# Two matmul orders changed: interleaved first tiles in the MLP's down stages, and the output stage's first row sums and projections placed behind the attention

## The chip, the cores and the metric

The kernel runs on one core of a Trainium2 chip. The metric is the device time of one execution in microseconds, the median over runs. Engines: TensorE (PE in the profile, its weight loads PEld), VectorE (DVE), ScalarE (ACT), GpSimd (POOL) and SyncE (SP), which issues the DMAs. They work in parallel, each through its own list in order, and wait for each other by semaphores.

## What is computed

One transformer block over 1024 tokens of width 1024 (float32), with 256 context tokens for keys and values only:

```python
sh1, sc1, g1, sh2, sc2, g2 = modulation(c, w_mod, b_mod)
mix_lat = concatenate([mla_latent(...), swa_latent(...)])   # 8 full heads, 8 windowed heads
x = x + g1 * (mix_lat @ w_out)
x = x + g2 * squared_relu_mlp(modulate(x, g_mlp, sh2, sc2), w_mlp1, w_mlp2)

def squared_relu_mlp(h, w1, w2):
    a = jax.nn.relu(h @ w1)
    return (a * a) @ w2
```

`modulate` is an RMS norm with a gain, times (1 + scale), plus shift. The softmax of the attention is divided by its row sum; the kernel does this late, on the mixed output.

## The kernel before, in words

Each float32 operand of the large products is split into a high and a low half (fp32r): high by ScalarE (a copy), low by VectorE (value minus high). A product takes three matmuls: high x high, high x low, low x high. PSUM has eight banks of 128 x 512.

**Attention** (`attention_phase`). Steps s = 0 to S - 1 (S = 96), the last 64 for the full heads: one head and one tile of 128 queries. In a step TensorE makes the scores (L1347), VectorE their negated maximum (L1542), ScalarE the exponentials (L1467), TensorE turns them (L1363, three fills of 4, 4 and 2 tiles, through the two banks TB = 0, 1), ScalarE and VectorE split each fill (L1453, L1548), and TensorE multiplies with the values (L1391, bank 7), once for two steps. The fills pass a ring of two banks: fill n waits for `emptied` n - 1. TensorE's list for step s: scores of s with the third fill of s - 2 between them, fills 0 and 1 of s - 1, half of the values of unit (s - 3) // 2.

**Row sums.** `rs` holds the reciprocal row sums of a token tile. GpSimd widens a tile's (`widen`, L1677), TensorE turns them (L1685, two banks of four transposes), VectorE multiplies the mixed output with them (`scale_mix`, L1690), ScalarE and VectorE split the product (`high_mix` L1695, `low_mix` L1700) and TensorE projects it (`project`, L1715, 2 halves of 24 matmuls). In the kernel before, tiles 0 and 1 are turned inside the attention's ring at steps S - 3 and S - 2 (`TURN`), which gives the ring four more slots; the first half of tile 0's projection stands in TensorE's list ahead of the last step's fills and the second half behind them. The reciprocals are ready in two groups (`full_sums`): tiles 0 and 1 at step S - 4, tiles 2 to 7 behind the last attention output.

**Output stage** (`out_phase`). For tile t TensorE's list is: turn the row sums of t + 2, project t + 1, turn the normed tile t (L1820). VectorE's list is: gate and residual of t (L1773, L1777), the norm, `scale_mix` and `low_mix` of t + 2, then gain, shift and low half of the normed tile (L1792 to L1798).

**MLP** (`mlp_phase`). FF = 4096 in 32 blocks of 128; 8 stages of FC = 4 blocks. A stage has four up products (L2045, 48 matmuls each over all 1024 tokens), and eight down products, one for each token tile t (`down`, L2059, 4 blocks x 3 x 2 halves = 24 matmuls). Between them ScalarE rectifies and squares (L1985, L1987), VectorE squares and takes the low half (L2009, L2012). Tile t of the down stage uses the bank pair DB[t % 2] and waits until VectorE has added tile t - 2's pair to the accumulator (`added`, L2028; `finished`, L2026, in the last stage). Tile 0 waits ahead of each block f for `a_ready` and `w2_ready` of that block. The middle six stages are a loop. GpSimd multiplies the second weights with the gate (L1955).

Of the kernel before, what the change touches and what calls it, by code (L numbers as in the profile page):

```python
# [1029 lines left out]
def attention_phase(nc, A, scr, Z, tok, prep, me):  # L1030
# [138 lines left out]
    def hi_count(s, k):  # L1169

        return fill0[s] + k + 1

    def turn_slot(s, f):

        return slot(s - 1, 1) + 1 + f
# [116 lines left out]
    def tensor():  # L1292
# [112 lines left out]
        def turn_sums(s, t):  # L1405

            for f in range(2):
                n = turn_slot(s, f)
                pe.wait_ge(emptied, n - 1)
                prep.turn_sums(ps[:, TB + n % 2, :], t, f).then_inc(filled, 1)  # L1410
# [39 lines left out]
    def scalar():  # L1450
# [36 lines left out]
        for s in range(S + 1):  # L1487
# [15 lines left out]
            else:  # L1503
# [24 lines left out]
    def vector():  # L1528
# [16 lines left out]
        def lo_fill(s, k):  # L1545
            dve.wait_ge(hi_ready, hi_count(s, k))
            hi, lo = hi_lo(s, k)
            V.tensor_tensor(lo, turned(s, k), hi.bitcast(F32), ALU.subtract).then_inc(emptied, 1)  # L1548
# [28 lines left out]
        def scale_mix(s, t):  # L1577

            for f in range(2):
                n = turn_slot(s, f)  # L1580
                dve.wait_ge(filled, n + 1)
                prep.scale_mix(ps[:, TB + n % 2, :], t, f).then_inc(emptied, 1)

        for s in range(S + 1):
# [28 lines left out]
            if s - 1 in TURN:  # L1613
                prep.low_mix(TURN[s - 1])
# [4 lines left out]
    me.turn_done, me.sums_done, me.out_done, me.units = (filled, turn_slot(S - 2, 1) + 1), (rs_ready, 2), out_done, U  # L1619
# [6 lines left out]
def out_phase(nc, A, scr, Z, att, mlp, me):  # L1626
# [19 lines left out]
    TB, BB = 0, (4, 7)  # L1646
    YB = (2, 5)
# [31 lines left out]
    def turn_sums(to, t, f):  # L1679

        if f == 0:
            pe.wait_ge(widened, t + 1)
        for c in range(4):
            k = 4 * f + c
            last = nc.tensor.transpose(to[:, c * P:(c + 1) * P], flat(rb[:, 2 * k:2 * k + 2, :]), ident[:, :])  # L1685
        return last

    def scale_mix(src, t, f):

        return V.tensor_tensor(mn[:, t % 2, 1, 4 * f:4 * f + 4, :], src.rearrange("p (k c) -> p k c", k=4),  # L1690
                               mix[:, 4 * f:4 * f + 4, tile(t)], ALU.mult)

    def high_mix(t):

        nc.scalar.activation(mT[:, t % 2, 0, :, :], mn[:, t % 2, 1, :, :], ACT.Copy).then_inc(m_hi, 1)  # L1695
# [7 lines left out]
    def project(t, half):  # L1703

        if half == 0:
# [3 lines left out]
            if t == 1:  # L1709
                pe.wait_ge(att.exped, att.steps)  # L1710
# [17 lines left out]
    def sync():  # L1728
        sp.wait_ge(att.out_done, att.units)
        sp.dma_start(g1[:, :, :], scr["mod"][0:1, 2 * D:3 * D].partition_broadcast(P).rearrange("p a (k c) -> p (a k) c", c=P)).then_inc(g1_loaded, 16)  # L1730
        for t in range(NB):
            if t == NB - 1:
                sp.wait_ge(spread, 2 * (NB - 2))
                mlp.sync_first()
# [4 lines left out]
    def gpsimd():  # L1739
        for t in range(2, NB):  # L1740
            if t == 2:
                pool.wait_ge(*att.turn_done)
                pool.wait_ge(*att.sums_done)
            else:
                pool.wait_ge(spread, 2 * (t - 2))
            widen(t)

    def scalar():
        for t in range(NB):
# [6 lines left out]
            if t + 2 < NB:  # L1756
                act.wait_ge(scaled, 2 * t + 2)
# [6 lines left out]
    def vector():  # L1764
        dve.wait_ge(columns, 48)
        link(V.tensor_scalar_add(mcol[:, 1, :], mcol[:, 1, :], 1.0))
        link(V.tensor_tensor(mcol[:, 1, :], mcol[:, 1, :], gcol[:, :], ALU.mult))
        dve.wait_ge(g1_loaded, 16)
        for t in range(NB):
# [13 lines left out]
            if t + 2 < NB:  # L1783
                for f in range(2):
                    dve.wait_ge(spread, 2 * t + f + 1)
                    scale_mix(ps[:, BB[f], :], t + 2, f).then_inc(scaled, 1)
# [14 lines left out]
    def tensor():  # L1801
        def spread_sums(t):

            for f in range(2):
                if t == 2 and f == 1:
                    pe.wait_ge(att.out_done, att.units)
                if t > 2:
                    pe.wait_ge(scaled, 2 * (t - 3) + f + 1)
                turn_sums(ps[:, BB[f], :], t, f).then_inc(spread, 1)

# [12 lines left out]
        pe.wait_ge(att.exped, att.steps)  # L1823
        for t in range(NB):
# [5 lines left out]
            else:  # L1830
                pe.wait_ge(gated, NB - 1)
# [3 lines left out]
        pe.wait_ge(scaled, 2 * (NB - 2))  # L1835
        mlp.up_half(1, 0)
        pe.wait_ge(gated, NB)
# [4 lines left out]
    me.widen, me.turn_sums, me.scale_mix, me.high_mix, me.low_mix, me.project = widen, turn_sums, scale_mix, high_mix, low_mix, project  # L1842
# [4 lines left out]
def mlp_phase(nc, A, scr, Z, o, out, me):  # L1847
# [189 lines left out]
    def tensor():  # L2037
# [11 lines left out]
        def down(n, t, g0, free):  # L2049
            b = DB[t % 2]  # L2050
            if free is not None:
                pe.wait_ge(*free)
            for f in range(FC):
                if t == 0:
                    pe.wait_ge(a_ready, g0 + f + 1)
                    pe.wait_ge(w2_ready, g0 + f + 1)
                for i, (x, w) in enumerate(((0, 0), (0, 1), (1, 0))):
                    for half in range(2):
                        last = nc.tensor.matmul(ps[:, b + half, :], aT[x][:, f, t * P:(t + 1) * P],  # L2059
                                                w2[w][:, f, half * BANK:(half + 1) * BANK],  # L2060
                                                start=(f == 0 and i == 0), stop=(f == FC - 1 and i == 2))
            last.then_inc(down_ready, 1)
# [3 lines left out]
        for t in range(NB):  # L2066
            down(t, t, 0, (o.scaled_h, 2 * NB) if t < 2 else (added, t - 1))
        with pe.Fori(1, NCH - 1) as ch:
            for f in range(FC):
                up(ch * FC + f, f)  # L2070
            for t in range(NB):
                down(ch * NB + t, t, ch * FC, (added, ch * NB + t - 1))
# [3 lines left out]
        for t in range(NB):  # L2076
            down(n0 + t, t, NF - FC, (added, n0 + t - 1) if t < 2 else (finished, 2 * t - 2))
# [138 lines left out]
```

## Time and profile before

| | us |
|---|---|
| median of 3 runs | 1503.82 (1502.24 to 1505.94) |
| the profiled execution | 1506.07 |
| its span, first to last instruction | 1504.2 |
| TensorE busy | 1409.5 (94%) |
| VectorE busy | 834.0 (55%) |
| ScalarE busy | 611.9 (41%) |
| GpSimd busy | 390.4 (26%) |
| down products, 1536 matmuls (L2059) | 351.6 |
| up products in the loop and tail, 1440 matmuls (L2045) | 327.8 |
| projections, 384 matmuls (L1715) | 91.9 |

The attention ends near 688 us of the span, the output stage near 800, and the MLP takes the rest. Busy time says how long an engine has work in it; what ends a wait is in the chain of waits and the timeline. TensorE's matmul durations overlap, so for it the distance between starts counts, and the granted clock (1.0 is 2.4 GHz, 0.5 is 1.2 GHz).

### The profile page before, as it was taken

What the parts mean: (1) busy time and instruction counts of PE and PEld (TensorE: products, weight loads), DVE (VectorE), ACT (ScalarE), POOL (GpSimd) and SP (SyncE); (2) the same over time, 40 slices, a digit from 0 to 9 for tenths busy, and PEclk for the clock granted to TensorE, in tenths of its full rate; (3) what the DMA queues carried; (4) which work ended last, traced back from release to release, by engine and by line L of the source; (5) the groups of instructions that cost most, each with busy time, mean ns of one, the idle gap of its engine ahead of it and who ended that gap; (6) DMA issues with size and microseconds to landing.
All of it is one profiled execution on the core that took longest, in us unless ns stands there. A gap on an engine that the chain in (4) does not pass through costs nothing.

```text
span 1504.2 us, 19176 instructions
## 1 busy us (share of the span) xinstructions
PE 1409.5 (94%) x7467; PEld 1186.4 (79%) x7467; DVE 834.0 (55%) x1143; ACT 611.9 (41%) x1194; POOL 390.4 (26%) x270
## 2 busy tenths in 40 slices
PE   3699997999999999988998999999999999999998
PEld 0488886888899998977877887887878788787887
DVE  1667786788788877864775325242343424344332
ACT  2455655777777787952223112030211203021120
POOL 4345653000099991301002111020110201011010
PEclk9999998999999999999999999999999999999999
DMA  9456657900156536201023111020201102011012
GB/s 332 136 146 175 177 149 242 276 12 1 66 165 204 161 115 178 66 1 55 30 70 98 42 56 57 28 84 0 84 28 47 65 13 91 8 58 53 28 56 98
DMA packets 123347, 141.03 MB, mean 94 GB/s; under 512 B 10224, under 2 KB 105216, under 8 KB 120464
## 3 DMA queue, kind: packets, MB, share of 16 engines
q1 hardware_dynamic: 122768, 140.08, 30.2%
q8 instruction: 44, 0.72, 0.2%
q14 instruction: 23, 0.19, 0.0%
q0 software_dynamic: 512, 0.04, 0.0%
HBM read 108.37 MB, written 31.74 MB: 93 GB/s over the span
## 4 chain that ended last, share of the span: by engine, by line
PE 71%; DVE 14%; ACT 9%; DMA 3%; issue 2%; SPq 1%; POOL 0%; DVEq 0%; ACTq 0%; POOLq 0%
PE f_ps L2045 22%; PE f_ps L2059 21%; PE a_ps L1347 7%; PE a_ps L1363 5%; PE a_ps L1391 5%; ACT s_pr L1459 2%; PE t_ps L923 2%; PE o_ps L1715 2%; DMA t_wm<-in_w_mod 2%; ACT s_pT L1453 2%; PE t_ps L912 2%; DVE f_aT L2012 1%; DVE s_nmx L1537 1%; PE t_ps L935 1%; DMA scratch_sv<-t_vs 1%
## 5 line engine op out<-in xcount | busy, mean ns | idle before, releaser
L2059 PE MATMUL f_ps<-f_w,f_aT 128*128 128x512 f32 x1536 | 351.6, 390 | 10.6 <-DVE f_aT L2012 9.8
L2059 PEld LDWEIGHTS f_ps<-f_w,f_aT 128*128 128x128 f32 x1536 | 287.8, 188 | 73.1 <-DVE f_aT L2012 12.3
L2045 PE MATMUL f_ps<-h,f_w 128*128 128x512 f32 x1440 | 327.8, 389 | 0.5 <-DVE f_w L1903 0.5
L2045 PEld LDWEIGHTS f_ps<-h,f_w 128*128 128x128 f32 x1440 | 270.2, 188 | 56.9 <-DVE f_w L1903 0.9
L1955 POOL TENSOR_TENSOR f_w2r<-f_w2r,f_g 128x1024 f32<-128x1024 f32 x32 | 81.6, 2550 | 620.2 <-DMA f_w2r<-in_w_mlp 620.2
L2028 DVE TENSOR_TENSOR mix<-mix,f_ps 128x512 f32<-128x512 f32 x112 | 71.9, 684 | 216.0 <-PE f_ps L2059 216.0
L2009 DVE TENSOR_TENSOR f_a<-f_r 128x1024 f32<-128x1024 f32 x32 | 55.5, 1735 | 187.2 <-ACT f_r L1985 187.2
L1972 ACT ACTIVATE f_w<-f_w2r 128x1024 fp32r<-128x1024 f32 x32 | 33.7, 1052 | 300.8 <-PE f_ps L2059 295.0
L1548 DVE TENSOR_TENSOR l_pT<-a_ps,l_pT 128x512 fp32r<-128x512 f32 (+1 forms) x192 | 108.9, 594 | 65.0 <-ACT l_pT L1453 65.0
L1347 PE MATMUL a_ps<-l_k,l_q 96*128 96x512 f32 (+1 forms) x576 | 136.4, 366 | 0.5 <-DVE l_mo L1569 0.5
L923 PE MATMUL t_ps<-w_in,t_h 128*128 128x416 f32 (+2 forms) x624 | 127.4, 350 | 1.5 <-DVE t_h L711 1.5
L1985 ACT ACTIVATE f_r<-f_ps 128x1024 f32<-128x1024 f32 x32 | 32.9, 1029 | 230.2 <-PE f_ps L2045 221.7
L1453 ACT ACTIVATE l_pT<-a_ps 128x512 fp32r<-128x512 f32 (+1 forms) x192 | 95.0, 525 | 54.1 <-PE a_ps L1363 53.9
L923 PEld LDWEIGHTS t_ps<-w_in,t_h 128*128 128x128 f32 x624 | 101.9, 189 | 7.8 <-issue 1.7
L1467 ACT ACTIVATE l_pr<-a_ps,l_nb 128x256 f32<-128x256 f32 (+1 forms) x128 | 100.6, 791 | 15.1 <-DVE l_nb L1542 12.7
L1347 PEld LDWEIGHTS a_ps<-l_k,l_q 96*128 96x128 f32 x576 | 95.3, 189 | 12.4 <-DVE l_mo L1569 0.7
L1542 DVE TENSOR_REDUCE l_nb<-a_ps 128x1 f32<-128x1280 f32 x64 | 94.9, 1482 | 4.0 <-PE a_ps L1347 3.6
L1363 PE MATMUL a_ps<-ident,l_pr 128*128 128x128 f32 x640 | 93.9, 275 | 3.0 <-DVE l_pT L1548 2.9
L1715 PE MATMUL o_ps<-o_w,o_mT 128*128 128x512 f32 x384 | 91.9, 399 | 2.6 <-DVE o_mT L1700 2.6
L1391 PE MATMUL a_ps<-l_pT,l_v 128*128 128x256 f32 x640 | 91.4, 290 | 2.0 <-DVE mix L1562 1.5
L1363 PEld LDWEIGHTS a_ps<-ident,l_pr 128*128 128x128 f32 x640 | 73.7, 140 | 18.3 <-DVE l_pT L1548 9.2
L1715 PEld LDWEIGHTS o_ps<-o_w,o_mT 128*128 128x128 f32 x384 | 73.1, 192 | 18.7 <-DVE o_mT L1700 3.5
(205 smaller groups left out, 1889.9 us busy)
## 6 DMA issues: line engine op xcount, KB each, us to landing
l_wg<-in_w_mod SPq DMA_DIRECT2D x8, 2048.0 KB, 8.5
f_w1r<-in_w_mlp SPq DMA_DIRECT2D x32, 512.0 KB, 4.0
f_w2r<-in_w_mlp SPq DMA_DIRECT2D x32, 512.0 KB, 4.5
t_wm<-in_w_mod SPq DMA_DIRECT2D x8, 1024.0 KB, 8.6
scratch_k<-t_kT SPq DMA_DIRECT2D x20, 384.0 KB, 4.4
l_k<-scratch_k SPq DMA_DIRECT2D x8, 960.0 KB, 10.6
scratch_q<-t_qT SPq DMA_DIRECT2D x16, 384.0 KB, 4.8
l_q<-scratch_q SPq DMA_DIRECT2D x8, 768.0 KB, 7.3
```

The lines of the kernel that those rows point to most:

```text
L923: ins = MM(ps[:, ZB + n % 2, 0:w], hT[a][:, k, :], w_in[x][:, k, ZC[c]], start=(k == 0 and i == 0), stop=(k == KC - 1 and i == 2))
L1347: last = MM(fps[:, a0:a0 + hi - lo], qT[b][:, a, qt * P:(qt + 1) * P], kT[b][:, w, lo:hi], start=(i == 0), stop=(i == 2))
L1363: last = nc.tensor.transpose(ps[:, TB + n % 2, c * P:(c + 1) * P], x, ident[:, :])
L1391: last = MM(ps[:, OB, 0:2 * P], vm[h % 2][:, t, :], flat(l_pT[half][:, u % 2, t, :, :]), start=(half == 0 and t == 0), stop=(half == 1 and ...
L1453: nc.scalar.activation(hi_lo(s, k)[0], turned(s, k), ACT.Copy).then_inc(hi_ready, 1)
L1467: nc.scalar.activation(l_pr[:, odd, lo:hi], fps[:, a0 + lo:a0 + hi], ACT.Exp, bias=nb[:, odd:odd + 1], accum_out=l_sums[:, i, m % NB, m // ...
L1542: V.tensor_reduce(nb[:, s % 2:s % 2 + 1], fps[:, (s % 2) * KALL:(s % 2 + 1) * KALL], AX.X, ALU.max, negate=True).then_inc(shift_ready, 1)
L1548: V.tensor_tensor(lo, turned(s, k), hi.bitcast(F32), ALU.subtract).then_inc(emptied, 1)
L1715: last = nc.tensor.matmul(ps[:, YB[t % 2] + half, :], mT[:, t % 2, a, k, :], w_out[w][:, k, half * BANK:(half + 1) * BANK], start=(k == 0 ...
L1955: nc.gpsimd.tensor_tensor(w2r[:, :], w2r[:, :], g2[:, :], ALU.mult).then_inc(w2_gated, 1)
L2045: last = nc.tensor.matmul(ps[:, b + half, :], w1[:, slot, w, k, :], h2[x][:, k, half * BANK:(half + 1) * BANK], start=(k == 0 and i == 0), ...
L2059: last = nc.tensor.matmul(ps[:, b + half, :], aT[x][:, f, t * P:(t + 1) * P], w2[w][:, f, half * BANK:(half + 1) * BANK], start=(f == 0 an ...
```

## The change

In the down stages (`down_first`) TensorE makes blocks 0 to 2 of tile 0, blocks 0 to 2 of tile 1, then block 3 of tile 0 and block 3 of tile 1. Tiles 2 to 7 are as before. Before block 3 it waits for the block's `a_ready` and `w2_ready` as before.

In the attention the two `TURN` insertions go, and with them the ring's four extra slots and tile 0's projection halves at the last step. Tile 0's row sums are turned behind the last third fill, ahead of the last values, into the output stage's own pair of banks 2 and 3 (`spread_sums(0)`). Tile 1's are turned behind the last values, and then tile 0 is projected in one piece, ahead of the output stage's loop. VectorE's and ScalarE's shares of tile 0 stand ahead of the last attention output, those of tile 1 behind the last reciprocals. Projections use the pairs 4, 5 and 6, 7 in place of 2, 3 and 5, 6. The numbers of some waits follow.

The core of the diff:

```diff
@@ attention_phase @@
-    TURN = {S - 3: 0, S - 2: 1}
     def slot(s, k):
-        return fill0[s] + k + sum(2 for x in TURN if x <= s or (x == s + 1 and k == 2))
+        return fill0[s] + k
@@ attention_phase, gpsimd @@
-        for t in range(2):
-            if t == 0:
-                pool.wait_ge(rs_ready, 1)
-            else:
-                pool.wait_ge(filled, turn_slot(S - 3, 1) + 1)
-            prep.widen(t)
+        pool.wait_ge(rs_ready, 1)
+        prep.widen(0)
@@ attention_phase, tensor @@
             else:
                 third_fill(s - 2)
-                pe.wait_ge(exped, S - 1)
-                prep.project(0, 0)
             if s and s != SUM_AT:
                 fill(s - 1, 0)
                 fill(s - 1, 1)
-            if s in TURN:
-                turn_sums(s, TURN[s])
             if s >= 3:
                 values((s - 3) // 2, 0 if s % 2 else 1)
-        prep.project(0, 1)
         third_fill(S - 1)
+        prep.spread_sums(0)
         values(U - 1, 0)
         values(U - 1, 1)
@@ attention_phase, scalar @@
-                if s - 1 in TURN:
-                    act.wait_ge(emptied, turn_slot(s - 1, 1) + 1)
-                    prep.high_mix(TURN[s - 1])
+        prep.high_mix(0)
         low(U - 1)
@@ attention_phase, vector @@
-                if s in TURN:
-                    scale_mix(s, TURN[s])
                 lo_fill(s - 1, 2)
...
-            if s - 1 in TURN:
-                prep.low_mix(TURN[s - 1])
+        prep.scale_mix(0)
+        prep.low_mix(0)
         out(U - 1)
         full_sums(2, NB)
@@ out_phase @@
-    TB, BB = 0, (4, 7)
-    YB = (2, 5)
+    TB, BB = 0, (2, 3)
+    YB = (4, 6)
...
+    def spread_sums(t):
+        pe.wait_ge(widened, t + 1)
+        for f in range(2):
+            if t:
+                pe.wait_ge(scaled, 2 * t - 1 + f)
+            for c in range(4):
+                k = 4 * f + c
+                last = nc.tensor.transpose(ps[:, BB[f], c * P:(c + 1) * P], flat(rb[:, 2 * k:2 * k + 2, :]), ident[:, :])
+            last.then_inc(spread, 1)
+
+    def scale_mix(t):
+        for f in range(2):
+            dve.wait_ge(spread, 2 * t + f + 1)
+            V.tensor_tensor(mn[:, t % 2, 1, 4 * f:4 * f + 4, :], bank(BB[f]), mix[:, 4 * f:4 * f + 4, tile(t)],
+                            ALU.mult).then_inc(scaled, 1)
...
@@ out_phase, tensor @@
-        pe.wait_ge(att.exped, att.steps)
+        spread_sums(1)
+        project(0, 0)
+        project(0, 1)
         for t in range(NB):
@@ mlp_phase, tensor @@
+        def down_part(t, f):
+            for i, (x, w) in enumerate(((0, 0), (0, 1), (1, 0))):
+                for half in range(2):
+                    last = nc.tensor.matmul(ps[:, DB[t % 2] + half, :], aT[x][:, f, t * P:(t + 1) * P],
+                                            w2[w][:, f, half * BANK:(half + 1) * BANK],
+                                            start=(f == 0 and i == 0), stop=(f == FC - 1 and i == 2))
+            if f == FC - 1:
+                last.then_inc(down_ready, 1)
+
+        def down_first(g0, free0, free1):
+            for t, free in ((0, free0), (1, free1)):
                 pe.wait_ge(*free)
+                for f in range(FC - 1):
+                    if t == 0:
+                        pe.wait_ge(a_ready, g0 + f + 1)
+                        pe.wait_ge(w2_ready, g0 + f + 1)
+                    down_part(t, f)
+            pe.wait_ge(a_ready, g0 + FC)
+            pe.wait_ge(w2_ready, g0 + FC)
+            for t in range(2):
+                down_part(t, FC - 1)
...
-            for t in range(NB):
-                down(ch * NB + t, t, ch * FC, (added, ch * NB + t - 1))
+            down_first(ch * FC, (added, ch * NB - 1), (added, ch * NB))
+            for t in range(2, NB):
+                down(t, (added, ch * NB + t - 1))
```

## Rows read from the trace of the kernel before

**Rows 1.** Part 1 of the page: busy time by engine, share, instructions.
```profile
PE 1409.5 (94%) x7467; PEld 1186.4 (79%) x7467; DVE 834.0 (55%) x1143; ACT 611.9 (41%) x1194; POOL 390.4 (26%) x270
```

**Rows 2.** The chain in order of time, MLP: start, us, what.
```profile
834.81 1.04 ACT f_r L1985
...
879.36 43.53 PE f_ps L2045 x192
...
968.34 43.53 PE f_ps L2045 x192
...
1456.79 43.53 PE f_ps L2059 x192
```

**Rows 3.** Timeline at a middle down stage: start, us, engine, line, operation, [idle before].
```profile
922.72 4.24 PE L2059 MATMUL f_ps<-f_w,f_aT 128*128 128x512 f32 x18
...
925.24 3.30 DVE L2012 TENSOR_TENSOR f_aT<-f_a,f_aT 128x1024 fp32r<-128x1024 f32 x1
...
928.59 5.74 PE L2059 MATMUL f_ps<-f_w,f_aT 128*128 128x512 f32 x24 [1.63 <-DVE f_aT L2012]
```

**Rows 4.** Timeline at the last down stage.
```profile
1456.63 43.68 PE L2059 MATMUL f_ps<-f_w,f_aT 128*128 128x512 f32 x192
...
1462.27 1.28 DVE L2026 TENSOR_TENSOR f_fin<-mix,f_ps 128x512 f32<-128x512 f32 x2 [1.90 <-PE f_ps L2059]
```

**Rows 5.** Timeline where GpSimd's product runs beside VectorE.
```profile
795.15 2.39 POOL L1955 TENSOR_TENSOR f_w2r<-f_w2r,f_g 128x1024 f32<-128x1024 f32 x1 [49.48 <-DMA f_w2r<-in_w_mlp]
795.16 0.69 DVE L1792 TENSOR_TENSOR o_hn<-o_ps,o_mcol 128x512 f32<-128x512 f32 x1 [0.16 <-PE o_ps L1820]
795.89 2.74 DVE L1795 TENSOR_TENSOR o_hn<-o_hn,o_mcol 128x1024 f32<-128x1024 f32 x1
```

**Rows 6.** Timeline of two regular attention steps.
```profile
644.16 0.86 PE L1347 MATMUL a_ps<-l_k,l_q 96*128 96x512 f32 x3
...
646.33 1.49 DVE L1542 TENSOR_REDUCE l_nb<-a_ps 128x1 f32<-128x1280 f32 x1
...
648.19 0.86 PE L1347 MATMUL a_ps<-l_k,l_q 96*128 96x512 f32 x3
...
648.32 1.11 ACT L1467 ACTIVATE l_pr<-a_ps,l_nb 128x1024 f32<-128x1024 f32 x1
```

**Rows 7.** Timeline of the attention's last steps.
```profile
653.18 1.25 PE L1685 MATMUL a_ps<-ident,o_rb 128*128 128x128 f32 x8 [1.97 <-DVE l_pT L1548]
...
659.79 1.25 PE L1685 MATMUL a_ps<-ident,o_rb 128*128 128x128 f32 x8 [1.30 <-DVE l_pT L1548]
...
660.48 1.29 DVE L1690 TENSOR_TENSOR o_mn<-a_ps,mix 128x512 f32<-128x512 f32 x2 [0.15 <-PE a_ps L1685]
...
668.24 0.44 PE L1363 MATMUL a_ps<-ident,l_pr 128*128 128x128 f32 x2 [1.97 <-DVE l_pT L1548]
...
668.44 7.33 PE L1715 MATMUL o_ps<-o_w,o_mT 128*128 128x512 f32 x24
...
677.68 5.63 PE L1715 MATMUL o_ps<-o_w,o_mT 128*128 128x512 f32 x24
...
685.01 2.62 PE L1391 MATMUL a_ps<-l_pT,l_v 128*128 128x256 f32 x20 [1.48 <-DVE mix L1562]
```

**Rows 8.** Timeline of the output stage's first tiles.
```profile
690.54 1.94 PE L1685 MATMUL o_ps<-ident,o_rb 128*128 128x128 f32 x8 [2.91 <-POOL o_rb L1677]
...
692.13 11.82 PE L1715 MATMUL o_ps<-o_w,o_mT 128*128 128x512 f32 x48
...
692.78 1.23 DVE L1773 TENSOR_TENSOR mix<-o_ps,o_g 128x1024 f32<-128x1024 f32 x1 [3.33 <-DMA o_g<-scratch_mod]
...
704.43 1.29 DVE L1792 TENSOR_TENSOR o_hn<-o_ps,o_mcol 128x512 f32<-128x512 f32 x2 [1.93 <-PE o_ps L1820]
...
704.66 1.04 PE L1685 MATMUL o_ps<-ident,o_rb 128*128 128x128 f32 x8
```

**Rows 9.** Busy time by engine in two microseconds; PEclk is TensorE's granted clock.
```profile
core 0: us, PE busy (x) PEld busy (x) DVE busy (x) ACT busy (x) POOL busy (x), PEclk, DMA share, GB/s
...
670.00:672.00 2.00, 2.00 (x6) 1.52 (x6) 1.24 (x2) 0.51 (x1) 0.00 (x0) 0.50 0.00 0
```

More of the change, by code:

```diff
@@ L1403, in sum_gate @@
             last.then_inc(gate_summed, 1)
[L1405 to L1410, printed above, removed]
         tok.tensor_over()
@@ L1545, in lo_fill @@
         def lo_fill(s, k):
-            dve.wait_ge(hi_ready, hi_count(s, k))
+            dve.wait_ge(hi_ready, slot(s, k) + 1)
             hi, lo = hi_lo(s, k)
@@ L1575, in full_sums @@
             V.reciprocal(rs[:, lo:hi, 0:HEADS], l_sums[:, 0, lo:hi, :]).then_inc(rs_ready, 1)
[L1577 to L1582, printed above, removed]
         for s in range(S + 1):
@@ L1618, in attention_phase @@
     me.w_lo = w_lo
-    me.turn_done, me.sums_done, me.out_done, me.units = (filled, turn_slot(S - 2, 1) + 1), (rs_ready, 2), out_done, U
+    me.sums_done, me.out_done, me.units = (rs_ready, 2), out_done, U
     me.exped, me.steps, me.emptied, me.fills = exped, S, emptied, slot(S - 1, 2) + 1
@@ L1677, in widen @@
         nc.gpsimd.tensor_copy(rb[:, :, :], bc(rs[:, t, :], VD)).then_inc(widened, 1)
[L1679 to L1691, printed above, removed]
+    def spread_sums(t):
[12 more added lines that the diff above has]
+                            ALU.mult).then_inc(scaled, 1)
     def high_mix(t):
+        act.wait_ge(scaled, 2 * t + 2)
         nc.scalar.activation(mT[:, t % 2, 0, :, :], mn[:, t % 2, 1, :, :], ACT.Copy).then_inc(m_hi, 1)
@@ L1709, in project @@
             if t == 1:
-                pe.wait_ge(att.exped, att.steps)
+                pe.wait_ge(att.out_done, att.units)
             if t >= 2:
@@ L1732, in sync @@
             if t == NB - 1:
-                sp.wait_ge(spread, 2 * (NB - 2))
+                sp.wait_ge(spread, 2 * NB)
                 mlp.sync_first()
@@ L1739, in gpsimd @@
     def gpsimd():
-        for t in range(2, NB):
+        for t in range(1, NB):
+            pool.wait_ge(spread, 2 * t)
             if t == 2:
-                pool.wait_ge(*att.turn_done)
                 pool.wait_ge(*att.sums_done)
-            else:
-                pool.wait_ge(spread, 2 * (t - 2))
             widen(t)
     def scalar():
+        high_mix(1)
         for t in range(NB):
@@ L1756, in scalar @@
             if t + 2 < NB:
-                act.wait_ge(scaled, 2 * t + 2)
                 high_mix(t + 2)
@@ L1767, in vector @@
         link(V.tensor_tensor(mcol[:, 1, :], mcol[:, 1, :], gcol[:, :], ALU.mult))
+        scale_mix(1)
+        low_mix(1)
         dve.wait_ge(g1_loaded, 16)
@@ L1783, in vector @@
             if t + 2 < NB:
-                for f in range(2):
-                    dve.wait_ge(spread, 2 * t + f + 1)
-                    scale_mix(ps[:, BB[f], :], t + 2, f).then_inc(scaled, 1)
+                scale_mix(t + 2)
                 low_mix(t + 2)
@@ L1801, in tensor @@
     def tensor():
[L1802 to L1809, printed above, removed]
         def turn(t):
@@ L1821, in turn @@
                 last.then_inc(turned, 1)
-        pe.wait_ge(att.exped, att.steps)
+        spread_sums(1)
+        project(0, 0)
+        project(0, 1)
         for t in range(NB):
@@ L1830, in tensor @@
             else:
-                pe.wait_ge(gated, NB - 1)
+                pe.wait_ge(scaled, 2 * NB)
                 pe.wait_ge(h_ready, NB // 2)
@@ L1834, in tensor @@
             turn(t)
-        pe.wait_ge(scaled, 2 * (NB - 2))
+        pe.wait_ge(gated, NB - 1)
         mlp.up_half(1, 0)
-        pe.wait_ge(gated, NB)
         pe.wait_ge(h_ready, NB)
@@ L1840, in tensor @@
         mlp.up_half(1, 1)
-    me.widen, me.turn_sums, me.scale_mix, me.high_mix, me.low_mix, me.project = widen, turn_sums, scale_mix, high_mix, low_mix, project
+    me.widen, me.spread_sums, me.scale_mix, me.high_mix, me.low_mix = widen, spread_sums, scale_mix, high_mix, low_mix
     me.sync_columns, me.sync, me.gpsimd, me.scalar, me.vector, me.tensor = sync_columns, sync, gpsimd, scalar, vector, tensor
@@ L2047, in up, with down @@
             last.then_inc(up_ready, 1)
-        def down(n, t, g0, free):
-            b = DB[t % 2]
-            if free is not None:
-                pe.wait_ge(*free)
-            for f in range(FC):
[L2054 to L2062, printed above, removed]
+        def down_part(t, f):
[8 more added lines that the diff above has]
+            for t, free in ((0, free0), (1, free1)):
+                pe.wait_ge(*free)
+                for f in range(FC - 1):
[7 more added lines that the diff above has]
+                down_part(t, FC - 1)
+        def down(t, free):
+            pe.wait_ge(*free)
+            for f in range(FC):
+                down_part(t, f)
         for f in range(2, FC):
             up(f, f)
-        for t in range(NB):
-            down(t, t, 0, (o.scaled_h, 2 * NB) if t < 2 else (added, t - 1))
+        down_first(0, (o.gated, NB), (o.scaled_h, 2 * NB))
+        for t in range(2, NB):
+            down(t, (added, t - 1))
         with pe.Fori(1, NCH - 1) as ch:
@@ L2070, in tensor @@
                 up(ch * FC + f, f)
-            for t in range(NB):
-                down(ch * NB + t, t, ch * FC, (added, ch * NB + t - 1))
+            down_first(ch * FC, (added, ch * NB - 1), (added, ch * NB))
+            for t in range(2, NB):
+                down(t, (added, ch * NB + t - 1))
         for f in range(FC):
@@ L2075, in tensor @@
         n0 = (NCH - 1) * NB
-        for t in range(NB):
-            down(n0 + t, t, NF - FC, (added, n0 + t - 1) if t < 2 else (finished, 2 * t - 2))
+        down_first(NF - FC, (added, n0 - 1), (added, n0))
+        for t in range(2, NB):
+            down(t, (finished, 2 * t - 2))
     me.sync_first, me.first_high, me.first_low, me.up_half = sync_first, first_high, first_low, up_half
```

4 lines of the change are left out of this document (removed).

## The prediction

> **What bounds the kernel now.** I read the page first: TensorE (PE) is busy for 94% of the span [rows 1], so what counts is where it stands still, or runs slowly, with nothing else to do. The chain in order of time then shows the MLP as an alternation of 43.53 us of up and about as much of down products [rows 2]. From one up stage to the next is 968.34 - 879.36 = 88.98 us, and the last down stage, the only one without a hole, takes 43.53 us. So a middle stage of the eight loses 88.98 - 2 x 43.53 = 1.92 us. The timeline says where: 18 matmuls (token tile 0, blocks 0 to 2) run, then TensorE stands for 1.63 us until VectorE (DVE) has written the low half of block 3, at 925.24 + 3.30 = 928.54, and starts again at 928.59 [rows 3]. It is the only hole in such a stage.
>
> The other weak place is the end of the attention. Its regular period is 648.19 - 644.16 = 4.03 us a step, and TensorE bounds it [rows 6]. Behind the first step with two fills for tile 0's row sums there are waits of 1.97 us ahead of these fills, 1.30 us at the second pair, 1.97 us at the third fill of step S-2, 1.48 us ahead of the last values and 2.91 us for GpSimd's widening of tile 2 [rows 7, 8]. The window at 670 shows TensorE's granted clock at 0.50, that is 1.2 of 2.4 GHz; the engine had stood still for most of the two microseconds from 666.3 to 668.2 before that [rows 7, 9]. The projection's half under it takes 7.33 us, where the other half takes 5.63 us [rows 7]: 1.7 us lost. The eight transposes at 690.54 take 1.94 us and the 48 matmuls behind them 11.82 us, about 1.5 us above their price at full clock (1.04 for eight at 704.66, and 2 x 5.6) [rows 7, 8].
>
> **Part 1, the down stages.** Tile 1's blocks 0 to 2 now stand between tile 0's block 2 and block 3. In the middle stages the cover of block 3's preparation grows from 18 to 36 matmuls, from 4.1 to 8.2 us (43.53 / 192 = 0.227 us a matmul). Wanted are 928.54 - 922.72 = 5.8 us [rows 3], so the wait goes, with 2.3 us to spare. Removed: six times 1.92 us, and in stage 0, which runs 879.36 - 834.81 = 44.55 us where 43.53 would do, 1.02 us [rows 2]. The last stage has no such wait. Together 11.5 + 1.0 = 12.5 us.
>
> What is late next is tile 2. It writes the banks of tile 0 and waits until DVE has added them to the accumulator. Before, a whole tile lay between (24 matmuls, 5.4 us); now tile 0 ends six matmuls ahead of tile 1 and only 6 x 0.227 = 1.36 us cover the additions. Their price: in the last stage the first addition starts 1462.27 - 1456.63 = 5.64 us behind the first matmul, thus 0.2 us behind the tile's nominal end of 5.44, and the pair takes 1.28 us [rows 4]. TensorE is let go at 0.2 + 1.28 + 0.05 = 1.53 us, where 1.36 is covered; the weight load that runs ahead of a matmul in a full pipe (some 0.2 us) then starts late too. I take 0.35 us a stage, eight times, last stage included: 2.8 us. Nothing shows this wait in the trace of before. Below there is nothing to gain (0); above I bound it by 0.8 us a stage, the 1.63 us hole halved, since that one also holds a whole DVE operation: 0 to 6.4 us. Tile 3 waits for tile 1's additions, which end long before (24 matmuls between). DVE is free then: its last operation ahead of the additions ends at 928.54 and block 3 of tile 0 would now end near 932.3.
>
> GpSimd's gating product could stretch the additions. The trace shows both cases: beside this product the operation with two SBUF inputs takes 2.74 us, but the one that reads PSUM keeps 0.69 us [rows 5]. The additions read PSUM, so I add nothing. The Trainium skill, "GPSIMD Engine Reference", section 8 (Key points), says that GpSimd shares its SBUF interfaces with VectorE, in contention with instructions of two SBUF inputs. By that rule the additions, with one SBUF input, stay at 1.28 us and the sum is the same; if it held for them too (2.7-fold) they would take 3.5 us, and tile 2's wait would be 2.5 us a stage. What follows does not rest on it.
>
> MLP: 12.5 - 2.8 = 9.7 us, range 6.1 to 12.5. The added waits on other semaphores (gated and scaled_h for the first stage, the earlier `added` counts) are passed long before.
>
> **Part 2, the output stage's head.** I walk from tick 648.19 (scores of step S-3) to 704.43, DVE's first product with tile 0's turned rows [rows 6, 8]: 56.2 us. Behind that point DVE's order, the counts it waits for and the banks' release are the same as before, so the remaining tiles and the first MLP blocks only move with it; the other banks cost nothing, since each reader still works on a pair that TensorE doesn't write.
>
> TensorE's work in the new order at full clock is 3 steps x 4.03 = 12.1; fills (ten transposes) 1.3; values 10 and 20 matmuls 1.2 + 2.6 [rows 7]; row-sum transposes for three tiles 3 x 0.95; two whole projections 2 x 11.2 (twice 5.63, less the overlap) [rows 7]; the first four transposes of turn 0 and the step to DVE 0.65. Sum 43.1.
>
> The waits that remain: the sums of two tiles still delay DVE at step S-3 (0.5). Behind the last scores TensorE must wait through the maximum 1.49, the low half of the fill 0.6 (third fill of S-2: 1.0 open), both exponentials (the longer 1.11 [rows 6]; 0.9 open), the third fill's low half (0.5), and ahead of the last values the attention output of the unit before (0.55). Then tile 0's chain: mix product 1.29 [rows 7], and a high and a low half of about 1.1 and 1.2 us, lie beside the last values (2.6) and tile 1's transposes (0.95): DVE is through at 671.0, TensorE at 671.05 in my walk, so open by 0.1 at most. GpSimd's widening of tiles 1 and 2 is hidden now: tile 2's had cost 2.91 us [rows 8], and has both halves of projection 0 (11.2 us) ahead of its reader. DVE's high and low mix for tile 1 is hidden too. The load of the gate row, for which DVE still waited 3.33 us at 692.78 [rows 8], is issued when the last attention output is through (671.4 in the walk); its reader comes at 682, some 10 us later. Sum of waits 3.6, so 46.7 us in place of 56.2: 9.5 us gained. Projection 0 no longer fills holes in the attention, but these holes came from TensorE's own detour.
>
> Clock: from 661 to 667 TensorE would be busy little more than half the time, though no single wait is above 1.0 us; before, it fell behind a wait of 1.97 us. I charge one fall, 1.7 us, in the projection or just ahead. Bounds: none (0) and both of before (3.2) with 1.5 us of slips in the walk. Part 2: 9.5 - 1.7 = 7.8 us, range 4.8 to 9.5.
>
> **Sum.** 9.7 + 7.8 = 17.5 us: span 1504.2 to 1486.7, the profiled execution 1506.07 to 1488.6. It lies 2.2 us above the median of three runs, 1503.82, so the prediction for the median is 1486.3 us (-1.2%).
>
> **Rivals.** (A) Tile 2's wait takes back most of the MLP's gain. For: the cover falls from 5.4 to 1.36 us against a need of 1.53; against: the additions have always the same length. It needs 12.5 / 8 = 1.57 us a stage to give all back; then 1503.8 - 7.8 = 1496 us. (B) The attention's last steps don't recover the 4.03 us period, and tile 0's serial chain lies open. For: the ring of two banks still joins TensorE, ScalarE and DVE; against: it kept 4.03 us with the same operations. Its price: values end at 687.6 - 12.6 (projection) - 2.5 (16 transposes) = 672.5; with 3 x 0.95, 22.4, 0.65 and 3.6 of chain + 1.0 of widening open, the mark is at 703.0. A gain of 1.4 in place of 7.8: 1492.7 us. (C) Slower: TensorE's clock falls in the thin stretch and stays at 1.2 GHz through both bare projections, which nothing interrupts but which now come straight behind it. Each of the 96 matmuls then costs 0.23 us more, 22.4 us; with the 1.7 already charged the time is 1507.0. The point from which it is slower than before is 38 us at the lower level. Against: the half that starts at 677.68, 9 us behind the fall, had its full-clock price again [rows 7]. The Trainium skill, "TensorE: Matmul & The Clock Gate", section "HAM oscillation", tells of kernels in which short bursts between waits are cold every time; by it each thin stretch is charged, which is the bound above, not the long stay. (D) The parts do little for a reason that I don't see, within 0.3%. That the first part misses its wait is excluded by 928.54 and 928.59.
>
> **Chances and range.** Forecast 0.74, A 0.10, B 0.08, D 0.04, C 0.04. Ends: 12.5 + 9.5 = 22 us and 6.1 + 4.8 = 10.9 us give 1481.8 to 1492.9; with 2 us for the scatter of medians (the three runs cover 3.7 us) 1480 to 1495, which takes in B and leaves out A's full size, C and D. About 0.3% (4.5 us) is what a measurement here can tell from no change: faster 0.92, same 0.05, slower 0.03.
>
> **What would show it.** In the MLP: an up stage starting every 87.4 us instead of 88.98; no wait on f_aT, but eight waits of 0.2 to 0.5 us on the accumulator's addition at tile 2. At the head: scores every 4.03 us up to the last step, DVE's first product with turned rows near 696 instead of 704.4, no wait on the widening, TensorE at half clock once and for about 3 us. It is wrong if tile 2's wait is above 0.8 us, if tile 0's projection starts later than 673, or if the output stage takes longer than before from tile 1 on.

## The result and the profile after

| | before | changed |
|---|---|---|
| median, us | 1504.88 (1502.24 to 1507.55) | 1480.95 (1480.62 to 1483.23) |
| ratio, 95% interval | | 0.9857 (0.9840 to 0.9875) |
| profiled execution, us | 1506.07 | 1481.20 |
| its span, us | 1504.2 | 1479.4 |

The changed kernel is 1.4% faster, 18.8 to 24.1 us. Timed once more on another occasion its ratio was 0.9873 (0.9855 to 0.9891), 16 to 22 us.

**Where it came from.** Four stretches of the two traces, cut at events that both have:

| stretch | before | changed | less |
|---|---|---|---|
| start to the scores of step S - 3 (unchanged code) | 648.19 | 643.99 | 4.2 |
| to VectorE's first product with turned rows (head) | 56.24 | 45.59 | 10.65 |
| to the end of stage 0's up products (output stage) | 130.4 | 130.0 | 0.35 |
| to the end of the span (MLP from its first down stage) | 669.4 | 659.8 | 9.6 |

The sum is 24.8 us, the difference of the spans. The chain in order of time of the changed kernel (start, us, what) at one middle stage and around it:

```profile
863.45 43.52 PE f_ps L2005 x192
...
916.71 0.51 issue
917.22 0.69 DVE mix L1988
...
917.95 32.94 PE f_ps L2012 x144
950.89 43.52 PE f_ps L2005 x192
```

Up stages now start 950.89 - 863.45 = 87.44 us apart, where it was 88.98 [rows 2]. The product on f_aT that used to end a wait has gone from the chain; in its place stands the accumulator's addition (L1988, L2028 in the kernel before) ahead of tile 2. In the timeline of the same stage (idle time before in brackets):

```profile
906.58 10.84 PEld L2012 LDWEIGHTS f_ps<-f_w,f_aT 128*128 128x128 f32 x48
...
909.33 3.31 DVE L1972 TENSOR_TENSOR f_aT<-f_a,f_aT 128x1024 fp32r<-128x1024 f32 x1
916.61 2.65 DVE L1988 TENSOR_TENSOR mix<-mix,f_ps 128x512 f32<-128x512 f32 x4 [3.98 <-PE f_ps L2012]
917.95 2.60 PEld L2012 LDWEIGHTS f_ps<-f_w,f_aT 128*128 128x128 f32 x12 [0.53 <-DVE mix L1988]
```

The slow low half of block 3 takes 3.31 us, as before [rows 3], but it ends at 912.64 while the weight loads run on until all 48 of two tiles are through. Then comes the new wait, 0.53 us of the weight load's queue. For the products of the down stages as a whole (who ended the idle time of TensorE or of its weight loads: us, times):

```profile
  DVE mix L1988: 3.6, 7
  DVE f_fin L1986: 0.4, 1
```

In stage 0, and only there, the additions ahead of tile 2 run beside GpSimd's product:

```profile
827.97 2.40 POOL L1915 TENSOR_TENSOR f_w2r<-f_w2r,f_g 128x1024 f32<-128x1024 f32 x1 [6.96 <-DMA f_w2r<-in_w_mlp]
829.17 2.64 DVE L1988 TENSOR_TENSOR mix<-mix,f_ps 128x512 f32<-128x512 f32 x4 [4.67 <-PE f_ps L2012]
```

The head, in the timeline of the changed kernel:

```profile
643.99 0.86 PE L1334 MATMUL a_ps<-l_k,l_q 96*128 96x512 f32 x3
...
648.98 0.44 PE L1350 MATMUL a_ps<-ident,l_pr 128*128 128x128 f32 x2
...
657.21 0.44 PE L1350 MATMUL a_ps<-ident,l_pr 128*128 128x128 f32 x2 [0.51 <-DVE l_pT L1522]
...
658.30 1.39 PE L1350 MATMUL a_ps<-ident,l_pr 128*128 128x128 f32 x8 [0.66 <-ACT l_pr L1443]
...
662.57 2.63 PE L1378 MATMUL a_ps<-l_pT,l_v 128*128 128x256 f32 x20 [0.60 <-DVE mix L1536]
...
666.15 10.76 PEld L1685 LDWEIGHTS o_ps<-o_w,o_mT 128*128 128x128 f32 x48 [0.31 <-DVE o_mT L1670]
666.15 11.18 PE L1685 MATMUL o_ps<-o_w,o_mT 128*128 128x512 f32 x48
...
689.58 1.29 DVE L1760 TENSOR_TENSOR o_hn<-o_ps,o_mcol 128x512 f32<-128x512 f32 x2 [1.96 <-PE o_ps L1779]
```

The four waits that are left are 0.5 to 0.7 us each (for the third fill of a step twice, the first of them, at 648.98, in the queue of weight loads; for the last exponentials; for the attention output ahead of the last values), and 0.31 us of the weight loads ahead of projection 0. Another 0.31 us of theirs lies inside the eight transposes at 658.30, which take 1.39 us in place of 1.04. The waits of 1.97, 1.30, 1.97, 1.48 and 2.91 us [rows 7, 8] have gone, and with them the slow projection [rows 7, 9]: in the busy time by engine, with PEclk third from the right, the granted clock is 1.00 also where TensorE has least to do.

```profile
core 0: us, PE busy (x) PEld busy (x) DVE busy (x) ACT busy (x) POOL busy (x), PEclk, DMA share, GB/s
656.00:660.00 4.00, 2.75 (x21) 2.07 (x20) 2.55 (x5) 3.06 (x8) 0.00 (x0) 1.00 0.00 0
660.00:664.00 4.00, 3.40 (x30) 3.19 (x29) 3.14 (x6) 1.31 (x4) 1.04 (x1) 1.00 0.00 0
```

And over the six microseconds in which the prediction had TensorE thinnest:

```profile
656.80:662.80 6.00, 4.26 (x32) 3.58 (x33) 3.95 (x8) 3.68 (x9) 0.77 (x1) 1.00 0.00 0
```

One longer wait stands in both kernels, and the change doesn't touch it. Near the end of the output stage TensorE waits 4.06 us for the last normed tile, and the clock falls there too: eight transposes take 1.97 us in place of 1.04. Before:

```profile
793.16 1.97 PE L1820 MATMUL o_ps<-ident,o_xn 128*128 128x128 f32 x8 [4.06 <-DVE o_xn L1782]
```

Changed, with the busy time of the two microseconds around the restart:

```profile
778.29 1.97 PE L1779 MATMUL o_ps<-ident,o_xn 128*128 128x128 f32 x8 [4.05 <-DVE o_xn L1752]
```

```profile
778.00:780.00 2.00, 1.71 (x9) 1.72 (x9) 2.00 (x3) 0.19 (x1) 0.17 (x1) 0.50 0.36 145
```

It is longer than any wait that this change removed.

### The profile page after: what moved, and what is told of

It reads as the page before. It is cut to its first block, busy times and chain, and to the rows that moved or that the text cites. A ratio compares the mean times of both kernels' runs of the same rounds, so it can differ in the third digit from the quotient of the medians.

```text
span 1479.4 us, 19175 instructions
## 1 busy us (share of the span) xinstructions
PE 1403.5 (95%) x7467; PEld 1182.9 (80%) x7467; DVE 838.1 (57%) x1143; ACT 611.8 (41%) x1194; POOL 389.0 (26%) x270
## 4 chain that ended last, share of the span: by engine, by line
PE 72%; DVE 12%; ACT 10%; DMA 3%; issue 2%; SPq 1%; POOL 0%; DVEq 0%; ACTq 0%
PE f_ps L2012 23%; PE f_ps L2005 22%; PE a_ps L1334 7%; PE a_ps L1350 5%; PE a_ps L1378 4%; ACT s_pr L1435 3%; PE t_ps L923 2%; PE o_ps L1685 2%; DMA t_wm<-in_w_mod 2%; ACT s_pT L1429 2%; PE t_ps L912 2%; DVE s_nmx L1511 1%; PE t_ps L935 1%; ACT l_pr L1443 1%; DVE l_nb L1516 1%
## 5 line engine op out<-in xcount | busy, mean ns | idle before, releaser
L1988 DVE TENSOR_TENSOR mix<-mix,f_ps 128x512 f32<-128x512 f32 x112 | 72.0, 684 | 205.8 <-PE f_ps L2012 205.2
L1969 DVE TENSOR_TENSOR f_a<-f_r 128x1024 f32<-128x1024 f32 x32 | 59.1, 1846 | 184.0 <-ACT f_r L1945 184.0
```

## The experiments

**Each part alone.** The kernel before with the down stages of the changed one, nothing else:

```diff
-        def down(n, t, g0, free):
...
+        def down_part(t, f):
...
+        def down_first(g0, free0, free1):
...
+        def down(t, free):
...
```

> The kernel before with the interleaved down stages alone. My theory: the two parts add, and this one gives 9.6 us (from the last up products of stage 0 to the end it measured 655.9 us after against 665.5 before): ratio 0.9936, up stages start every 87.44 us, head as before (TensorE's clock falls once at 670). Rival (the parts help each other, for instance through the clock): less than 7 us alone.

Measured: ratio 0.9949 (0.9932 to 0.9966), span 1493.9. Stages at 87.44 us:

```profile
877.97 43.52 PE f_ps L2045 x192
...
965.42 43.52 PE f_ps L2045 x192
```

From the end of stage 0's up products (834.12) to the end it is 659.8 us, as in the changed kernel: 9.6 us less than before. The rest of its trace is 0.7 us shorter than before: 2.2 us less ahead of the first sums, 1.3 us more in the head and 0.2 us more in the output stage. The head's code is the same. TensorE's clock fell at the same two waits as before, but the second time for longer.

```profile
668.00:670.00 2.00, 2.00 (x6) 1.59 (x5) 1.23 (x1) 0.31 (x1) 0.00 (x0) 0.50 0.00 0
...
688.00:690.00 2.00, 1.68 (x9) 1.71 (x9) 0.00 (x0) 0.00 (x0) 0.17 (x1) 0.50 0.96 274
690.00:692.00 2.00, 2.00 (x7) 1.61 (x6) 1.44 (x2) 0.00 (x0) 1.04 (x1) 0.50 0.37 150
692.00:694.00 2.00, 2.00 (x6) 1.52 (x6) 1.02 (x1) 0.95 (x1) 0.00 (x0) 0.50 0.00 0
```

The first fall is like that of before. The second holds 0.50 from 688 to 694, six microseconds, where the transposes and the projection of before lost 1.5 us in all [rows 8]. So the old head costs a varying amount. The ratio of this run stands for 7.7 us (5.1 to 10.2), which has the expected 9.6 in its interval; the two medians differ by 9.7.

The other part alone: the changed kernel with the old down stages.

```diff
-        def down_part(t, f):
...
-        def down_first(g0, free0, free1):
...
-        def down(t, free):
...
+        def down(n, t, g0, free):
...
```

> The changed kernel with the old order of the down stages: the head part alone. My theory: 56.2 us from the scores of step S-3 to VectorE's first product with turned rows become 45.6, a gain of 10.6 us, ratio 0.993; down stages at 88.98 us. The 4.2 us by which the changed kernel's trace already lay earlier ahead of step S-3, in code that is the same, is scatter of the loads and belongs to neither part. Rival: the head's change moves something earlier as well, and the span ahead of S-3 is again 4 us shorter: then ratio 0.990.

Measured: ratio 0.9931 (0.9915 to 0.9947), which is 10.4 us (8.0 to 12.8). From the first sums of `full_sums` on VectorE to its first product with turned rows the trace has 43.06 us, the changed kernel 43.05, the kernel before 53.70: a gain of 10.64 us. The MLP takes 669.4 us from its first down stage, as before. The first sums stand here:

```profile
649.62 0.17 DVE L1548 TENSOR_TENSOR l_sums<-l_sums 128x16 f32<-128x16 f32 x1
...
692.68 1.29 DVE L1760 TENSOR_TENSOR o_hn<-o_ps,o_mcol 128x512 f32<-128x512 f32 x2 [1.96 <-PE o_ps L1779]
```

The kernel before had them at 650.73, the changed one at 646.53, and the eight further traces of this study between 647.1 and 649.6. The front of the rival, 4 us shorter, did not come: this part of the trace difference is scatter of code that nothing changed, and the gain of the two parts is 10.65 + 0.35 + 9.6 = 20.6 us. In the traces the two parts add exactly; the ratios add within their intervals (0.9949 x 0.9931 = 0.9880, the two comparisons of the changed kernel 0.9857 and 0.9873).

The ten traces also say where the scatter lies. It is there by 312 us of the span; from there to the scores of step S - 3 TensorE's matmuls keep their distance in all ten within 0.2 us. And 1.2 to 1.7 us of it are TensorE's clock, which stands at 0.50 for a part of the stretch from 240 to 280 us, for longer in some traces than in others. The kernel before:

```profile
240.00:280.00 40.00, 29.88 (x165) 26.07 (x164) 25.69 (x43) 21.96 (x46) 6.80 (x9) 0.74 0.95 311
```

The changed kernel:

```profile
240.00:280.00 40.00, 28.67 (x172) 24.66 (x170) 27.24 (x48) 23.19 (x50) 6.80 (x9) 0.83 0.99 321
```

Four traces have 0.74 there (the kernel before, its variant with the projection moved, and both of the last variant below), six have 0.83, and neither head has only the one or the other.

**What in the head.** The kernel before with tile 0's projection behind the last values, the row sums still turned inside the ring:

```diff
                 third_fill(s - 2)
-                pe.wait_ge(exped, S - 1)
-                prep.project(0, 0)
...
-        prep.project(0, 1)
         third_fill(S - 1)
         values(U - 1, 0)
         values(U - 1, 1)
+        prep.project(0, 0)
+        prep.project(0, 1)
```

> The kernel before with tile 0's projection moved behind the last values, and the row sums of tiles 0 and 1 still turned inside the attention's ring. It tells the two halves of the head part apart. My theory (the ring's extra slots cost the most, and the projection inside the attention's end stands ahead of fills that others wait for): the steps S-2 and S-1 stay 6.6 to 7.1 us apart from the next, but the stretch from the last scores to the last values falls from 22.9 us to some 11; with 11.2 us of projection behind it the mark moves earlier by 1 to 4 us against before. Rival (the projection filled holes that cost nothing otherwise, and the gain is all of the ring's): the mark is later than before by 3 us or more, since the holes of 1.5 and 2 us and the wait for the widening stay and nothing fills them.

Measured: ratio 0.9971 (0.9958 to 0.9983); from the first sums to the first product with turned rows 51.20 us, 2.5 less than before, 8.15 more than changed. So the theory's gain of 1 to 4 us came, and not the rival's loss. From the last scores to the last values it is 12.7 us where some 11 were expected; 1.6 us of them are the second fall of the clock described below. TensorE's timeline:

```profile
651.91 1.85 PE L1684 MATMUL a_ps<-ident,o_rb 128*128 128x128 f32 x8 [1.98 <-DVE l_pT L1547]
...
659.91 1.25 PE L1684 MATMUL a_ps<-ident,o_rb 128*128 128x128 f32 x8 [1.31 <-DVE l_pT L1547]
...
668.36 0.44 PE L1363 MATMUL a_ps<-ident,l_pr 128*128 128x128 f32 x2 [1.98 <-DVE l_pT L1547]
669.45 1.97 PE L1363 MATMUL a_ps<-ident,l_pr 128*128 128x128 f32 x8 [0.66 <-ACT l_pr L1466]
671.07 2.10 PE L1391 MATMUL a_ps<-l_pT,l_v 128*128 128x256 f32 x10
...
674.86 2.63 PE L1391 MATMUL a_ps<-l_pT,l_v 128*128 128x256 f32 x20 [1.47 <-DVE mix L1561]
677.33 11.07 PE L1714 MATMUL o_ps<-o_w,o_mT 128*128 128x512 f32 x48
```

The waits of 1.98, 1.31, 1.98 and 1.47 us are those of before; they belong to the ring's slots and not to the projection. Taken as a filler, the projection had hidden none of them, and only the 0.66 us for the last exponentials that shows at 669.45. What its move gives is the wait for the widening of tile 2 (2.91 us [rows 8]), which runs beside it in this variant. The eight transposes at 651.91 and the values at 671.07 run at a lower clock (1.85 for 1.25 us, 2.10 for 1.43 us), so the clock fell here too, twice, and once already behind the first wait of 1.98 us, which in the trace of before had no such effect. Of the head's 10.65 us about a quarter (2.5 us) is the projection's place. The other 8.15 us are the rest of the head's edits together: the ring's slots, the places where the rows of tiles 0 and 1 are turned, and the new bank pairs. No run takes these apart; that most of it is the ring's is read from its waits. Divided by kind and not by edit, 3.2 us of the 10.65 are the clock (1.7 and 1.5 us before [rows 7, 8], no fall now) and some 7 us are waits: 9.6 us of them before, less than 3 now.

**How near the clock is.** The changed kernel with three useless additions on VectorE ahead of tile 0's low half:

```diff
         prep.scale_mix(0)
+        prep.hold()
         prep.low_mix(0)
...
+    def hold():
+
+        for i in range(3):
+            link(V.tensor_tensor(xn[:, :, :], mix[:, :, tile(0)], mix[:, :, tile(0)], ALU.add))
```

> The changed kernel with three useless VectorE additions (1.25 us each) ahead of tile 0's low half, beside ScalarE's high half: TensorE stands still 2.6 to 2.9 us ahead of projection 0, where it stood 0.3. It asks how near the changed head is to a fall of TensorE's clock. My theory: this wait brings the fall that the kernel before had, and costs the wait and about 1.7 us of slow projection: the mark (VectorE's first product with turned rows) is 4.0 to 4.6 us later, with a granted clock of 0.5 for some microseconds. Rival (the fall before came of the thinner stretch from 651 to 668 as a whole, with three waits, and one wait of this length does not do it): 2.7 us later and the clock at 1.00 throughout.

Measured: 47.24 us in place of 43.05, 4.2 more, where the theory had 4.0 to 4.6; ratio 0.9903 (0.9879 to 0.9928).

```profile
670.69 12.81 PE L1693 MATMUL o_ps<-o_w,o_mT 128*128 128x512 f32 x48 [2.64 <-DVE o_mT L1678]
```

```profile
670.00:672.00 2.00, 1.31 (x4) 1.10 (x5) 1.87 (x6) 0.00 (x0) 0.05 (x1) 0.82 0.00 0
672.00:674.00 2.00, 2.00 (x6) 1.53 (x5) 1.33 (x3) 0.60 (x1) 0.99 (x1) 0.50 0.53 205
674.00:676.00 2.00, 2.00 (x8) 1.59 (x8) 1.23 (x1) 0.46 (x1) 0.00 (x0) 0.82 0.79 318
```

The wait of 2.64 us in place of 0.31 is the only thing in the head that differs from the changed kernel; the other waits are the same. The clock is at 1.2 GHz within a microsecond or so of the restart, and the 48 matmuls take 12.81 us instead of 11.18: 1.6 us, the size of the fall before [rows 7]. The rival falls: one long wait on top of the thin stretch is enough. Whether the same wait would do it in a dense stretch, this run doesn't show.

**The price of tile 2's wait.** The changed kernel with tile 0's pair released only one matmul ahead of tile 1's end:

```diff
-        def down_part(t, f):
+        def down_part(t, f, held=0):
...
-            if f == FC - 1:
+                    if held == 2 and i == 2 and half == 0:
+                        last.then_inc(down_ready, 1)
+            if f == FC - 1 and held != 1:
                 last.then_inc(down_ready, 1)
...
-                down_part(t, FC - 1)
+                down_part(t, FC - 1, held=t + 1)
```

> The changed kernel with tile 0's pair released to VectorE only one matmul ahead of tile 1's end: the cover of the two additions falls from six matmuls to one. My theory: need 1.53 us and late restart against cover, so the wait at tile 2 grows from 0.38 by 5 x 0.227 = 1.13 to 1.5 us; stages every 88.6 us; 9 us slower than the changed kernel, about as slow as the old order. Rival (the wait at tile 2 is a fixed price of the semaphore, not of the additions): stages stay within 0.3 us of 87.44.

Measured: median 1492.8 us, ratio 0.9935 (0.9911 to 0.9959).

```profile
866.45 43.52 PE f_ps L2005 x192
...
955.02 43.52 PE f_ps L2005 x192
```

```profile
920.75 2.48 DVE L1988 TENSOR_TENSOR mix<-mix,f_ps 128x512 f32<-128x512 f32 x4 [5.11 <-PE f_ps L2012]
922.09 1.91 PEld L2012 LDWEIGHTS f_ps<-f_w,f_aT 128*128 128x128 f32 x9 [1.66 <-DVE mix L1988]
```

Stages take 955.02 - 866.45 = 88.57 us, 1.13 more than in the changed kernel: exactly the five matmuls of cover that were taken (5 x 0.227). The wait is the additions' time less the cover, and not a fixed price of the semaphore. From the end of stage 0's up products to the end it is 668.9 us, 9.1 more than changed, where 9 were expected. Both kernels give the same whole need, counted from a stage without any wait (87.04 us, below): 1.36 of cover + 0.40 lost, and 0.23 + 1.53, both 1.76 us, or eight matmuls.

**The cover doubled.** Two blocks of tile 1 behind tile 0's last block:

```diff
-                for f in range(FC - 1):
+                for f in range(FC - 1 - t):
...
-            for t in range(2):
-                down_part(t, FC - 1)
+            down_part(0, FC - 1)
+            down_part(1, FC - 2)
+            down_part(1, FC - 1)
```

> The changed kernel with two blocks of tile 1 behind tile 0's last block instead of one: tile 0's blocks 0 to 2, tile 1's 0 and 1, tile 0's block 3, tile 1's 2 and 3. Cover of block 3's preparation 30 matmuls, 6.8 us, against 5.84 wanted in the trace of the changed kernel; cover of the additions 12 matmuls, 2.7 us, against 1.5. My theory: both waits are gone, stages every 87.06 us (2 x 43.53), 8 x 0.37 = 3.0 us faster than the changed kernel. Rival: the preparation, 3.31 us beside GpSimd's product, is not ready at 6.8 us, and a hole comes back at block 3: no gain or a loss.

Measured: median 1480.91 us, ratio 0.9857 (0.9837 to 0.9877), no lower than the changed kernel had in another comparison. The trace says otherwise:

```profile
865.01 43.52 PE f_ps L2005 x192
908.53 43.52 PE f_ps L2012 x192
952.05 43.52 PE f_ps L2005 x192
```

No wait is left between stages, each is 43.52 us, 87.04 for two, and from the end of stage 0's up products (821.49) to the end it is 656.7 us against 659.8. A repeat of both on one chip decided:

> The changed kernel once more, beside the variant with two blocks of tile 1 behind tile 0's last, so that both are timed on one chip. Theory: 0.9850 of the kernel before in this comparison too, 43.05 us from the first reciprocal sums to VectorE's first product with turned rows, stages at 87.44 us; the span ahead of the first reciprocal sums anywhere between 646 and 651 us, since in seven traces of unchanged code it was. Rival (it is the changed head that makes the front shorter): 646.5 again.

Measured: median 1483.68 us (1482.05 to 1484.87), ratio 0.9873 (0.9855 to 0.9891), a little above the expected 0.9850. Head 43.08 us, stages at 87.44, first sums at 647.10.

> The variant with two blocks of tile 1 behind tile 0's last, again, beside the changed kernel. Its trace had stages at 87.04 us and 2.8 us less from the first reciprocal sums to the end, but the medians of two separate comparisons were the same (1480.9). Theory: on one chip it is 3.1 us below the changed kernel (ratio to before lower by 0.002). Rival: the medians agree within 1 us, and what the stages give is lost outside them.

Measured: median 1479.97 us (1479.61 to 1480.99), ratio 0.9849 (0.9835 to 0.9864). It is 3.7 us below the changed kernel on the same chip, and the two ranges don't touch; the theory had 3.1. The two traces are 2.8 us apart: 3.1 less in the MLP, 1.1 less in the output stage, where the clock's fall at the end lasted longer in this trace of the changed kernel, nothing in the head, and 1.45 more ahead of the first sums. So the 3.1 us are shown by the traces, and the other 0.6 of the medians are not assigned. The first comparison had shown no difference. Its trace has the first sums at 648.10, 1.6 us later than the changed kernel's 646.53, which hides half of the 3.1 us; in its other executions this wasn't seen. This version beats both kernels: 22.7 us, 1.5%, below the one before.

## Why the prediction was right

The median was 1480.95 us where 1486.3 was predicted, inside 1480 to 1495 but near its low end. The low end of the two parts alone was 1481.8; only the 2 us allowed for scatter took the measured time in, so that it lies inside is in part luck. The mechanisms are another matter. Point by point:

- **The hole at block 3.** Right in place and size: it is gone in all stages, and the up stages start 87.44 us apart, where 87.4 was foretold.
- **The new wait at tile 2.** Right: eight waits, 3.6 + 0.4 = 4.0 us of the weight loads' idle time in all (the prediction had foretold 0.2 to 0.5 us each), which costs 87.44 - 87.04 = 0.40 us a stage in the period, where 0.35 was taken. The MLP gave 9.6 us for 9.7. Rival A is excluded by the traces; the held release shows by which mechanism it would have come.
- **GpSimd beside VectorE.** Right, but hardly put to the test. In the middle stages the product has ended (near 911.6) when the additions begin (916.61). Only in stage 0 does it run beside them, from 827.97 to 830.37, which covers the first two of the four additions, and the four take 2.64 us, as long as elsewhere.
- **The walk through the head.** 46.7 us were foretold without a fall of the clock, 45.6 measured. The order of waits was right; they were shorter than walked, about 0.5 us at the third fill of S - 2 instead of 1.0, 0.7 instead of 0.9 at the exponentials, and none instead of 0.5 at the last third fill. The scores of the last steps stand 4.05 and 4.46 us apart, the second with the delay by the sums of two tiles that the walk had (0.5). Rival B (the period not recovered, the chain open) didn't come: the wait ahead of projection 0 was 0.31 us. That the other bank pairs cost nothing was argued and fits the 45.6 us, but no run has them alone.
- **The clock.** This is the term that failed. I charged one fall, 1.7 us, because TensorE would be busy little more than half the time from 661 to 667, which is 656.8 to 662.8 in the changed kernel's trace. It was busy for 4.26 of these 6 us, and the clock stayed at 1.00. The run with one wait of 2.64 us shows what brings a fall here, a single long wait. The longest in the changed head is 0.7 us, and by the walk none was above 1.0, which should have weighed more than the busy share. The prediction also read only half of its own rows: it says that the clock fell behind a wait of 1.97 us, but the first such wait, ahead of 653.18, did nothing (the eight transposes behind it take 1.25 us, as those at 659.79) [rows 7]. Rival C fell with the term.
- **What was not in the sum.** 4.2 us of the difference of the two traces lie ahead of every changed line, more than 1 us of it in the longer time at half clock between 240 and 280 us. Scatter of this size also moves medians: the changed kernel's were 1480.95 and 1483.68 us. I had allowed 2 us for it.
- **What hides the widening.** Right, and worth 2.9 us: the variant with the projection behind the last values shows it alone.

So the error of 5.4 us in the median is 2.8 of the head (1.1 in the walk, 1.7 for the clock) and 0.35 between head and MLP. The remaining 2 us are smaller than the scatter of the front; that they are this scatter is likely, not shown.

## What to carry to other kernels

When a wait is filled by work of the next item, ask at once what that work pushes together at its other end: the pair of banks that is written and read again needs a cover as long as its evacuation and the late restart (here 1.76 us, eight matmuls), and the best split is found by writing both needs down (5.8 us ahead of block 3, 1.76 us behind tile 0) and giving each its cover. Work put into a ring of two buffers to use its gaps takes the ring's slots, and every user behind it waits for the round trip: four waits of 1.3 to 2.0 us here for two tiles, and a fall of TensorE's clock with them. A gain of 3 us in 1480 needs both versions on the same chip, or the trace cut at an event behind the part that scatters. And when the waits that a change is about are gone, list those that are left: one of 4.06 us, with a fall of the clock, stands in all ten traces at the end of the output stage.

## What the runs showed of the hardware

- TensorE's granted clock fell to 0.50 around every long wait of the ten traces behind the first 400 us: 2.64, 2.91 and 2.92 us in the heads, and 4.05 to 4.06 us at the end of the output stage in all ten. Of the six waits of 1.97 to 1.99 us it fell at four, and it did not fall at any of 1.15 to 1.67 us (the holes of the old down stages among them). So near 2 us it is open: at the first such wait it fell in the variant with the projection moved and not in the kernel before, though their code is the same up to there.
- The fall began between 1.0 us before TensorE's work started again and 1.4 us after it (clock 0.66 from 687 to 688 in the run with the down stages alone, work at 688.32; before, full until 669.6, work at 668.24). In the heads it cost 1.5 to 1.7 us of matmul time where it lasted between 3 and 4 us, as most did; three of all lasted nearly 7 us.
- VectorE's low half of block 3 (a subtraction of two operands in SBUF, 128 x 1024) took 3.31 us beside GpSimd's product, where 1.22 us is usual. What counts is which began first. In the traces of the kernel before and of the changed one, a low half, a square or a shift of VectorE began 45 times while GpSimd's product was under way. Each time it ended 1.08 to 1.09 us behind the product's end, for example 925.24 + 3.30 = 928.54 against 924.69 + 2.77 = 927.46. In the 16 cases where VectorE began first it took its usual 1.22 to 1.23 us. VectorE's additions that read PSUM kept 0.68 to 0.69 us beside the product.
- The stretch of unchanged code ahead of the first sums took 646.5 to 650.7 us in ten traces, and the scatter arises ahead of 312 us.
